# Token mixing written as one walk over half-units, its index, norm and attention steps put between the projections; the depthwise taps multiplied on ScalarE and summed on GpSimd

## What is computed

```python
z = h @ w_in + b_in
u_pool, u_conv, q, k, v, qi, ki, wi, gates = split_cols(z, IN_SIZES)   # 256, 512, 512, 128, 128, 512, 64, 8, 3072 columns
q, k, qi, ki = rope(q), rope(k), rope(qi) * 64 ** -0.5, rope(ki)
y_pool = pool_mixer(u_pool, pool_w, pool_scale) @ w_pool_out
h = a * sigmoid(gate)                                  # a, gate = halves of u_conv
h = causal_dwconv(h, dw_w, dw_b)                       # 31 taps, 256 channels
y_conv = silu(layer_norm(h, ln_g, ln_b)) @ w_conv_out
score = einsum('bqsh,bqh->bqs', relu(qi . ki), wi)     # 8 index heads, 256 x 256, causal
idx = top_k(score, 64)                                 # each query attends to its 64 best keys
y_attn = softmax_attention(q, k[idx], v[idx]) @ w_attn_out   # 8 heads of 64
g = sigmoid(gates)                                     # three times 1024
out = (g[0] * y_pool + g[1] * y_conv + g[2] * y_attn) @ w_o
```

## Time and profile before

| | |
|---|---|
| device time, median of 3 | 2376.83 us (2375.1 to 2379.86) |
| span of the profiled execution | 2375.4 us |
| PE, DVE, ACT, POOL busy | 2243.2, 1568.6, 1123.2, 388.0 us |
| first mixing layer, from its first matmul to the end of `w_o` | about 1483 to 1726.5 us of the span |
| second mixing layer | about 1930 to 2173.6 us |

### The profile page before, as it was taken

One profiled execution on the slowest core, in us unless ns is written; L12 is line 12 of the kernel. 1 busy time (PEld: TensorE's weight loads), 2 busy tenths in 40 slices (PEclk: granted clock), 3 DMA queues, 4 the chain that ended last, 5 costly groups with the idle time before them and its releaser, 6 DMA issues.

```text
span 2375.4 us, 43374 instructions
## 1 busy us (share of the span) xinstructions
PE 2243.2 (94%) x17246; PEld 2127.2 (90%) x17246; DVE 1568.6 (66%) x2061; ACT 1123.2 (47%) x1447; POOL 388.0 (16%) x456
## 2 busy tenths in 40 slices
PE   8999998999999999999999998978999989888998
PEld 7899998799999999999989996977799878867996
DVE  6865547656467776654786555768677667767775
ACT  5653345543345555433564434435365443444553
POOL 0012100021000000220301111660011229200221
PEclk9999998999999999999999999988999999989999
DMA  6356542366544445565435664534357544425663
GB/s 206 123 151 186 190 148 95 94 165 189 192 155 145 142 146 156 160 187 185 155 125 149 179 212 150 152 95 153 109 158 207 195 120 133 159 71 155 183 211 107
DMA packets 432651, 367.81 MB, mean 155 GB/s; under 512 B 20733, under 2 KB 404353, under 8 KB 432521
## 3 DMA queue, kind: packets, MB, share of 16 engines
q1 hardware_dynamic: 430744, 364.56, 49.8%
q0 software_dynamic: 1264, 0.71, 0.1%
q10 hardware_dynamic: 512, 0.72, 0.1%
HBM read 364.89 MB, written 1.05 MB: 154 GB/s over the span
## 4 chain that ended last, share of the span: by engine, by line
PE 76%; DVE 12%; POOL 6%; ACT 3%; issue 2%; DMA 0%; SPq 0%; ACTq 0%; DVEq 0%; POOLq 0%
PE bank L512 68%; POOL hT L1491 4%; DVE weights_lo L2069 4%; POOL Z L1493 2%; PE bank L543 1%; PE bank L908 1%; DVE Z L2663 1%; DVE h_lo L2641 1%; ACT weights_hi L1529 1%; DVE Z L2713 1%; PE bank L1103 1%; PE bank L1135 1%; PE bank L821 1%; PE bank L1116 1%; PE bank L922 1%
## 5 line engine op out<-in xcount | busy, mean ns | idle before, releaser
L2069 DVE TENSOR_TENSOR weights_lo<-weights,weights_hi 128x2048 fp32r<-128x2048 f32 x343 | 804.5, 2346 | 454.7 <-ACT weights_hi L1529 452.0
L512 PE MATMUL bank<-h_hi,weights_hi 128*128 128x256 f32 x3520 | 1008.2, 286 | 38.0 <-DVE h_lo L2641 17.3
L512 PE MATMUL bank<-h_lo,weights_hi 128*128 128x256 f32 x3520 | 996.7, 283 | 0.0
L512 PE MATMUL bank<-h_hi,weights_lo 128*128 128x256 f32 x3520 | 996.6, 283 | 0.0
L1529 ACT CAST weights_hi<-weights 128x2048 fp32r<-128x2048 f32 x343 | 654.5, 1908 | 527.8 <-PE bank L512 518.9
L512 PEld LDWEIGHTS bank<-h_hi,weights_hi 128*128 128x128 f32 x3520 | 677.0, 192 | 49.1 <-issue 36.4
L512 PEld LDWEIGHTS bank<-h_lo,weights_hi 128*128 128x128 f32 x3520 | 677.0, 192 | 1.5 <-issue 1.4
L512 PEld LDWEIGHTS bank<-h_hi,weights_lo 128*128 128x128 f32 x3520 | 676.2, 192 | 0.0
L1425 POOL CAST hid_hi<-hT 128x256 f32 (+1 forms) x132 | 52.4, 397 | 1515.9 <-DVE hT L2572 1098.7
L512 PE MATMUL bank<-hid_lo,weights_hi 128*128 (+1 forms) x528 | 147.6, 280 | 0.0
L512 PE MATMUL bank<-hid_hi,weights_hi 128*128 (+1 forms) x528 | 147.6, 280 | 0.0
(11 more groups left out here) (368 smaller groups left out, 3135.2 us busy)
## 6 DMA issues: line engine op xcount, KB each, us to landing
weights<-in_f_w_gu SPq DMA_DIRECT2D x176, 512.0 KB, 4.9
weights<-in_f_w_out SPq DMA_DIRECT2D x88, 512.0 KB, 4.2
weights<-in_w_up SPq DMA_DIRECT2D x88, 512.0 KB, 4.8
weights<-in_w_in SPq DMA_DIRECT2D x82, 512.0 KB, 4.4
weights<-in_c_w_qkv SPq DMA_DIRECT2D x72, 512.0 KB, 4.4
weights<-in_a_w_qkv SPq DMA_DIRECT2D x48, 512.0 KB, 4.6
weights<-in_w_down SPq DMA_DIRECT2D x44, 512.0 KB, 4.4
weights<-in_a_w_o SPq DMA_DIRECT2D x16, 512.0 KB, 4.1
```

Source lines behind the costliest of these rows:

```text
L512: mm = nc.tensor.matmul(out, x, y, start=(first and n == 0), stop=(last and n == 2), skip_group_check=True)
L2069: v_.tensor_tensor(w_lo[slot][:], raw[slot][:], w_hi[slot][:].bitcast(F32), ALU.subtract).then_inc(lo_ready, 1)
```

## The change

All four programs of `mix` now walk the same list, `M_UNITS`, in **half-units** t = 0 to 47 (unit n is t = 2n and 2n+1; a half-unit is 24 matmuls). After each half-unit PE calls `between(t)`, which looks up in tables what goes there: rotations at t = 6 to 20, one index head at each of t = 11 to 18, the pooling product at 22, the four norm steps at 28 to 31, attention heads from 32 to 45 (scores at t, scaling at t+1, transposes at t+2, values at t+3). ACT and DVE walk the same t. The gates' loop is gone: its twelve units stand in line, and the pool output's unit stands between gate 7 and gate 8.

The taps change engines. ACT multiplies (`tap`, both halves of the channels, two activations a tap) into a ring of four buffers; POOL adds (one 128 x 512 sum for each of taps 1 to 30). Tap j on ACT waits for the sum of tap j-4; the sum waits for its tap and for the sum before. DVE's `convolve` is gone. Masking and row maximum of a head are now one instruction for each 128 queries (a TENSOR_TENSOR_REDUCE, printed as ISA) in place of a SCALAR_TENSOR_TENSOR and a TENSOR_REDUCE. Gates 4 to 10 are evicted without the sigmoid, which follows at t = 43 and 44 in two large activations. The two attention output units are interleaved by bank, so that the four banks are complete one after the other.

```diff
@@ -87,6 +87,25 @@
+M_UNITS = (["conv_a", "conv_g", "ki", "qi0", "qi1", "vw", "pool", "k", "q0", "q1"] + [("gate", g) for g in range(8)]
+           + ["pool_out"] + [("gate", g) for g in range(8, 12)] + ["conv_out"])
+M_TURNED = ("ki", "qi0", "qi1", "k", "q0", "q1")
+M_ROT_AT = {6: 0, 8: 1, 10: 2, 16: 3, 18: 4, 20: 5}
+M_IDX_AT = {11 + hd: hd for hd in range(8)}
+M_TAPS_AT = {}
+for _j in range(31):
+    M_TAPS_AT.setdefault(6 + _j // 5 * 3 + (_j % 5) // 2, []).append(_j)
+M_POOLS, M_POOLMIX, M_POOLSPLIT = 15, 22, 23
+M_SEARCH = range(22, 31)
+M_CLN = 28
+M_SIGMOID_TO = 4
+M_SCORES_AT = {32: 0, 33: 1, 35: 2, 36: 3, 38: 4, 39: 5, 41: 6, 42: 7}
+M_SCALE_AT = {s + 1: hd for s, hd in M_SCORES_AT.items()}
+M_TURN_AT = {s + 2: hd for s, hd in M_SCORES_AT.items()}
+M_VALUES_AT = {s + 3: hd for s, hd in M_SCORES_AT.items()}
+M_MASK_AFTER = 24
...
@@ -1212,113 +1178,178 @@
...
-                pe.wait_ge(rot_ready, count(rot_ready, 3))
-                it["idx"] = []
-                for hd in range(IDX_HEADS):
-                    s = open_item([0, 2, 3, 6][hd % 4])
...
+                def index_scores(hd):
+
+                    pe.wait_ge(rot_ready, rot0 + 2 + hd // 4)
+                    s = open_item(4 + hd % 4)
...
-                with pe.Fori(0, rounds) as i:
-                    for j, u in enumerate(loop_units(lambda r, j: block_loads("w_in_2", l, r * 768 + (Z_GATE + j * 256)), 3, (0, rounds), 3)):
...
-                attn_64(tag, N_HEADS,
...
+                def conv_norm(step):
+
+                    if step == 0:
+                        pe.wait_ge(conv_step, count(conv_step, CONV_W - 1))
+                        x = open_item(2)
+                        close(stats(2, 0, conv_y, range(2)), x)
+                    elif step == 1:
+                        pe.wait_ge(bank_free[2], cln[0].free)
+                        x = open_item(3, released=False)
+                        close(spread(3, 0, 0), x)
...
+                def scores(hd):
+
+                    pe.wait_ge(rot_ready, rot0 + 6)
+                    a = HD * (hd % 2)
...
+                def turn(hd):
+
+                    pe.wait_ge(probs_ready, count(probs_ready))
+                    TT[hd] = open_item(6)
...
+                def between(t):
+
+                    if t in M_ROT_AT:
+                        k = M_ROT_AT[t]
+                        r = open_item(2 + k % 2)
+                        rotation(r, it[M_TURNED[k]], 2, n=2 * T if k else T)
+                        rr.append(r)
+                    if t in M_IDX_AT:
+                        index_scores(M_IDX_AT[t])
+                    if t == M_POOLMIX:
+                        pool_weights()
+                    if t in range(M_CLN, M_CLN + 4):
+                        conv_norm(t - M_CLN)
+                    if t in M_SCORES_AT:
+                        scores(M_SCORES_AT[t])
+                    if t in M_TURN_AT:
+                        turn(M_TURN_AT[t])
+                    if t in M_VALUES_AT:
+                        values(M_VALUES_AT[t])
...
+                    for half in range(2):
...
+                        elif n:
+                            mm = tiles([halves(x.bank)[half]], w, ((HD if kind == "k" else P) * half,), h)
+                        if half and n:
+                            close(mm, x, u)
+                        if kind == "vw":
+                            it["v"] = x
+                        between(2 * n + half)
...
+                out, held = [], [next_unit(deep_loads("w_attn_out_2", l, 2 * z)) for z in range(2)]
+                for m, z in ((0, 0), (1, 0), (0, 1), (1, 1), (2, 0), (3, 0), (2, 1), (3, 1)):
+                    if z == 0:
...
@@ -1480,27 +1511,22 @@
...
-                        else:
-                            gp.tensor_scalar(hT[:, 2 + j % 2, :], hh, wj, None, ALU.mult).then_inc(conv_step, 1)
-                            pool.wait_ge(conv_step, done)
-                            gp.tensor_tensor(conv_y[:, 0, :], conv_y[:, 0, :], hT[:, 2 + j % 2, :], ALU.add).then_inc(conv_step, 1)
+                    for j in range(1, CONV_W):
+                        pool.wait_ge(tap_ready, l * CONV_W + j + 1)
+                        if j > 1:
+                            pool.wait_ge(conv_step, l * (CONV_W - 1) + j - 1)
+                        gp.tensor_tensor(conv_y[:], tapM[0] if j == 1 else conv_y[:], tapM[j % 4], ALU.add).then_inc(conv_step, 1)
+                        if j == M_MASK_AFTER:
+                            for tt in range(NT):
+                                pool.wait_ge(score_step, IDX_HEADS * NT * seen_m + NT * (IDX_HEADS - 1) + tt + 1)
+
+                                gp.affine_select(out=score[:, tt, :], in_=score[:, tt, :], compare_op=ALU.is_ge,
+                                                 fill=FILL, base=tt * P, pattern=[[-1, T]],
...
@@ -1921,62 +1900,119 @@
...
+                def tap(j):
+
+                    if j == 0:
+                        act.wait_ge(glu_ready, l + 1)
+                        act.wait_ge(residual_ready, 2 * l + 1)
+                    if j >= 4:
+                        act.wait_ge(conv_step, l * (CONV_W - 1) + max(j - 4, 1))
+                    for m in range(2):
+                        hh = conv_h[:, m, PADW - CONV_W + 1 + j:PADW - CONV_W + 1 + j + T]
+                        ins = fn(tapM[j % 4][:, m, :], hh, ACT.Identity, scale=pcol[:, cw + 2 * j + m:cw + 2 * j + m + 1],
+                                 bias=eps[:, 3:4] if j else pcol[:, cb + m:cb + m + 1])
+                    ins.then_inc(tap_ready, 1)
+
+                for t_ in range(2 * len(M_UNITS)):
+                    n, half = t_ // 2, t_ % 2
+                    if half:
+                        evict(M_UNITS[n])
+                    if t_ in M_IDX_AT:
+                        hd = M_IDX_AT[t_]
+                        s = it["idx"][hd]
+                        done(s)
+                        if hd >= 2:
+                            act.wait_ge(score_step, NT * IDX_HEADS * l + 2 * (hd - 1))
+                        free(fn(relu[hd % 2], banks[s.bank][:], ACT.Relu, scale=HD ** -0.5), s)
+                    for j in M_TAPS_AT.get(t_, ()):
...
+                    if t_ == 43:
+                        fn(gates[:, 8:16, :], gates[:, 8:16, :], ACT.Sigmoid).then_inc(gates_ready, 1)
+                    if t_ == 44:
+                        fn(gates[:, 16:22, :], gates[:, 16:22, :], ACT.Sigmoid).then_inc(gates_ready, 1)
...
@@ -2648,24 +2635,6 @@
...
-                def convolve():
-
-                    dve.wait_ge(glu_ready, l + 1)
-                    for j in range(CONV_W):
-                        hh = conv_h[:, 1, PADW - CONV_W + 1 + j:PADW - CONV_W + 1 + j + T]
-                        elif j < CONV_W - 1:
-                            link(v_.scalar_tensor_tensor(y, hh, wj, y, ALU.mult, ALU.add))
-                        else:
-                            v_.scalar_tensor_tensor(y, hh, wj, y, ALU.mult, ALU.add).then_inc(conv_out, 1)
-                        if j % 2:
-                            yield
-
...
+                def mask_scores(hd):
+
+                    if hd == 0:
+                        dve.wait_ge(keep_ready, count(keep_ready, NT))
+                    if hd >= 4:
+                        done(TT[hd - 4])
+                    done(S[hd])
+                    for tt in range(NT):
+                        ins = v_.tensor_tensor_reduce(expoM[hd % 4][:, tt * T:(tt + 1) * T], work[:, tt, :],
+                                                      banks[S[hd].bank][:, tt * T:(tt + 1) * T], 1.0, 3.0e38,
+                                                      ALU.add, ALU.min, negmax[hd % 4][:, tt:tt + 1])
+                    free(ins, S[hd])
...
+                for t_ in range(2 * len(M_UNITS)):
+                    n, half = t_ // 2, t_ % 2
+                    if t_ in M_ROT_AT:
+                        k = M_ROT_AT[t_]
+                        rotate(k, it[M_TURNED[k]], it["rot"][k], dsts[k], tabd[:, 0, :], tabd[:, 1, :], tiles=2 if k else 1)
+                    if t_ in M_IDX_AT:
+                        accumulate(M_IDX_AT[t_])
+                    if t_ == M_POOLS:
                         pools()
...
+                    if t_ in range(M_CLN, M_CLN + 5):
+                        conv_norm(t_ - M_CLN)
...
+                    if t_ in M_SCORES_AT:
+                        mask_scores(M_SCORES_AT[t_])
+                    if t_ in M_SCALE_AT:
+                        normalise(M_SCALE_AT[t_])
+                    if half == 0 and n:
+                        refill(us[n - 1])
+                    if t_ in M_SEARCH:
+                        for _ in range(2):
+                            next(search, None)
```

660 lines of the change are left out of this document (289 added, 371 removed).

## The result

The changed kernel takes 2339.38 us, median of 4 runs (2337.55 to 2345.24), beside 2378.35 us (2375.1 to 2380.83, 4 runs) for the kernel before on the same chip: ratio 0.9836, 95% interval 0.9818 to 0.9854. It is 39 us faster (1.6%); the forecast was 58. The time lies within the range of 2300 to 2343 us, near its upper end, and outside the forecast's own bounds of 2307 to 2333.

The account below looks back on a forecast made before the run. PE was taken as the bound, busy 2243.2 of 2375.4 us. Per layer 38 us to be had less a residue of 9 gives 29, 58 for both: span 2317.4, median 2319 us, range 2300 to 2343.

Parts of the forecast that it names:

- The 38 us a layer to be had: First mixing layer: PE's idle and half-clock time in four windows, together 33 to 44 us, taken as 38 a layer.
- the four stretches named: Index heads 8.0 to 10.8 us, search start 6.6 to 9.8, norm and attention 14.0 to 17.6, turn to `w_o` 4.3 to 6.0.
- The residue of 9: Loss left in each layer: 6 us of PE idle plus 3 for small waits and a half-clock stretch.
- 6 us at about t = 29: PE's spread in the norm waits for DVE: 9 us late less 2.8 of cover, bounds 0 and 16.
- hidden behind the slots: Each `weights_lo` stands on DVE at t = 2n+2, needed at 2n+6, so 9 us of DVE lag cost PE nothing.
- If every piece is ready in time, these are all that the moved steps cost: PE's moved pieces at full clock cost their listed times, index head 1.05, attention head 2.7, and the 38 us go.
- the excluding rival: DVE and POOL exclude each other whole: 19 us late, residue 19, gain 19 a layer, 2339 us; chance 0.22.
- the two bounds: Taps' stretch, t = 6 to 23: DVE and POOL nothing late if short instructions overlap, 19 us if none; 9 taken.
- The rule that I named as a rival: A DVE instruction with two SBUF inputs and a GpSimd one reading SBUF exclude each other wholly: 2339 us, chance 0.22.
- the one with everything hidden: DVE and POOL overlap as the index sums do, only 3 us of small waits stay: 35 a layer, 2307 us; chance 0.22.
- their chain would not set the pace: Rival that ACT's taps waiting for POOL's sums set the pace, 3.7 us a tap, 2399 us, had chance 0.06.
- the 0.9 of my count: Taps on ACT, t = 6 to 23: 31 pairs of activations at 0.9 us each, 28 us.

Follow-up runs that it names:

- e1: The changed kernel with the eight index heads put in as four pairs of different row halves instead of one by one: 2340.8 us.
- e4: The changed kernel with GpSimd's tap sums over 8 of 256 columns, the first sum whole, so the output is another: 2329.7 us.
- e9: The changed kernel with the taps put back as before on GpSimd and DVE, none on ACT, the half-unit walk kept: 2345.6 us.

## Why the prediction was right and wrong

**The 38 us a layer to be had: right.** Idle time and half clock came down from 45.8 to 18.8 us a layer, and the four stretches named are the ones that went: the index heads run without idle time before them, the attention heads at clock 1.00, and PE's idle time from 1666.6 us into `w_o` is 0.2 us.

**The residue of 9: right in size and place, by two errors that offset each other.** Behind the entrance PE waits 3.5 for `weights_lo`, 2.9 for `rs` at t = 29, 0.6 at `hT`, and 3.4 us of half clock follow: 10.4. I had put 6 us at about t = 29 and nothing ahead of it; between t = 22 and 29 PE's waits came to 6.2, but more than half of that for `weights_lo`, which I had hidden behind the slots, and 1.6 of it at t = 22, inside the taps' stretch. DVE was held longer than I allowed. Had PE's own work up to there been what I counted, its waits would have been longer by about as much: e1 took 4.6 us off its own work, and none off the time. That the 9 came out is in part luck.

**The step that failed** is "If every piece is ready in time, these are all that the moved steps cost". PE's own work grew by 8.6 us a layer. Some 3.5 is the lost overlap of the index heads, priced at 1.05 each from an attention head that stood alone, though in their row they cost 0.58 or less; 1.3 to 1.5 is overlap that attention's own heads had before. The rest, 3.6, is change-over, 0.09 to 0.20 us for each place between projections, which the sum left at nothing. With the second layer it makes 17 us, nearly all of the 19. The time lies in the stated range only because the range reached up for the excluding rival; by the sum alone it would have been missed.

**DVE and POOL: between the two bounds, nearer the late one.** GpSimd's sums took 1281 to 3372 ns, 1.86 us in the mean, where one alone takes 1.30. Long subtractions held them as the earlier trace rows had it (3.1 to 3.4 us), and short instructions with two SBUF inputs doubled as well (1335 for 692 ns). The earlier trace rows with 0.62 an index sum had misled me, since there POOL ran products of 128x256 in good part. The rule that I named as a rival ("SBUF — State Buffer", "Who interferes with whom" in the Trainium skill) is borne out for instructions that take two inputs from SBUF; the search's MAX8 (0.43 beside a sum) and the product with an input from PSUM (0.68) were not slowed, which fits it too. But as I had told it, it is too narrow: the cast and the TENSOR_SCALAR with one tensor input were held as well (1522 for 427 ns, 864 for 350). The rival's number, 2339 us, came true, its mechanism only in part: without contention the kernel takes 2329.7 (e4), so it cost 10 us and not the 32 that lie between that rival and the one with everything hidden, 2307. PE's own work, 17 us, is the larger part of those 32.

**The taps: right that their chain would not set the pace**, and no wait of PE was for an ACT held by taps. A tap's two activations took 1.09 us and not the 0.9 of my count, so ACT carried 34 us of taps instead of 28, and GpSimd waited 12.4 us for them between 1515 and 1600 us; neither reached PE. What I did not say is how little their move was worth, 6 us at most (e9).

**Open** is what the parts of the change other than the taps are worth one by one, and how the change-overs would sum in another order: their sizes were read from the timeline, no run changed their number alone.

## What to carry to other kernels

Price a moved instruction where it will stand, not where it stood. Here two heads in different halves ran at once, and that gain went when they were drawn apart; keep such neighbours in pairs. Every change of kind between long runs of matmuls cost something too (0.09 to 0.20 us), so where PE sets the pace a few larger pieces are better than many small ones. Before a saving on one engine is counted, look whether another has idle time left in the same window; where it has none (33.38 of 34 us), move work of that engine first, past the next thing that is waited for.
